# A two-layer hybrid decoder trunk: the post-norms' means taken in two fp32r parts, one small projection tile later, and ScalarE's copies of small tiles moved one place ahead

## The reference

```python
for i in range(DEPTH):
    h = rmsnorm(x, norm_pre[i])
    ...
    x = x + rmsnorm(y, norm_post[i])
    gate = jax.nn.sigmoid(rmsnorm(x, pe_norm[i]) @ pe_w_gate[i])
    x = x + gate * (p[i] @ pe_w_proj[i])
```

## Time and profile before

| | us |
|---|---|
| median of 3 runs | 633.39 (633.24 to 633.53) |
| the profiled execution, its own time | 633.8 |
| its span, first to last instruction | 631.8 |
| TensorE busy | 625.2 (99%) |
| VectorE, ScalarE, GpSimd busy | 391.8, 324.6, 297.7 |
| granted TensorE clock, mean | 1.000 of full speed |

### The profile page before, as it was taken

One profiled execution on the slowest core, in us unless ns is written; L12 is line 12 of the kernel. 1 busy time (PEld: TensorE's weight loads), 2 busy tenths in 40 slices (PEclk: granted clock), 3 DMA queues, 4 the chain that ended last, 5 costly groups with the idle time before them and its releaser, 6 DMA issues.

```text
span 631.8 us, 9261 instructions
## 1 busy us (share of the span) xinstructions
PE 625.2 (99%) x2924; PEld 516.2 (82%) x2924; DVE 391.8 (62%) x787; ACT 324.6 (51%) x562; POOL 297.7 (47%) x400
## 2 busy tenths in 40 slices
PE   8999999999999999999999999999999999999997
PEld 6788888888888887888888888888888888888886
DVE  5688777787868787555969635432424243357874
ACT  7766666565657575565666632321222222566451
POOL 1785463645555457000447458546553742002570
PEclk9999999999999999999999999999999999999999
DMA  6344333434335434155103323323223331352031
GB/s 208 108 161 120 117 130 119 114 114 116 115 121 108 102 104 149 34 166 168 33 25 109 101 75 123 106 95 128 71 98 101 100 133 67 116 184 67 1 133 67
DMA packets 26585, 68.03 MB, mean 108 GB/s; under 512 B 3504, under 2 KB 9648, under 8 KB 26560
## 3 DMA queue, kind: packets, MB, share of 16 engines
q1 hardware_dynamic: 26560, 67.71, 33.6%
HBM read 65.57 MB, written 2.13 MB: 107 GB/s over the span
## 4 chain that ended last, share of the span: by engine, by line
PE 96%; DVE 1%; DMA 1%; issue 1%; ACT 1%; SPq 0%; DVEq 0%
PE ps_pj L1115 26%; PE ps_pj L1117 26%; PE ps_pj L1116 26%; PE ps_tr L1124 3%; PE ps_o L1251 2%; PE ps_sc L1215 2%; PE ps_o L1250 1%; PE ps_sc L1213 1%; PE ps_pj L1152 1%; PE ps_tr L1115 1%; PE ps_tr L1117 1%; PE ps_tr L1116 1%; PE ps_pj L1146 1%; PE ps_pj L1145 1%; DMA xT<-in_xT 1%
## 5 line engine op out<-in xcount | busy, mean ns | idle before, releaser
L431 POOL TENSOR_TENSOR w_lo<-w_raw,w_hi 128x256 fp32r<-128x256 f32 x316 | 242.9, 801 | 129.7 <-ACT w_hi L493 120.9
L1115 PE MATMUL ps_pj<-act_hi,w_hi 128*128 128x512 f32 (+1 forms) x712 | 281.2, 395 | 0.0
L1117 PE MATMUL ps_pj<-act_hi,w_lo 128*128 128x512 f32 (+1 forms) x712 | 276.2, 388 | 0.0
L1116 PE MATMUL ps_pj<-act_lo,w_hi 128*128 128x512 f32 (+1 forms) x712 | 276.0, 388 | 0.0
L1117 PEld LDWEIGHTS ps_pj<-act_hi,w_lo 128*128 128x128 f32 x712 | 133.7, 188 | 27.8
L1115 PEld LDWEIGHTS ps_pj<-act_hi,w_hi 128*128 128x128 f32 x712 | 133.9, 188 | 25.4 <-DVE act_lo L928 0.4
L1116 PEld LDWEIGHTS ps_pj<-act_lo,w_hi 128*128 128x128 f32 x712 | 134.0, 188 | 23.9
L493 ACT CAST w_hi<-w_raw 128x1024 fp32r<-128x1024 f32 x95 | 99.4, 1048 | 87.9 <-DMA w_raw<-in_weights 65.5
L470 POOL TENSOR_TENSOR acc<-acc,sq 128x512 f32<-128x512 f32 x14 | 22.4, 1598 | 116.5 <-ACT sq L661 116.2
L439 POOL TENSOR_TENSOR bias<-bias,mask 128x128 f32<-128x128 f32 x60 | 30.7, 542 | 69.4 <-DMA bias<-negc_scratch 69.4
L563 ACT ACTIVATE logit<-logit,nmax 128x128 f32<-128x128 f32 (+1 forms) x64 | 36.1, 563 | 46.7 <-DVE nmax L828 46.4
(11 more groups left out here) (164 smaller groups left out, 776.4 us busy)
## 6 DMA issues: line engine op xcount, KB each, us to landing
w_raw<-in_weights SPq DMA_DIRECT2D x100, 512.0 KB, 3.3
bias<-negc_scratch SPq DMA_DIRECT2D x15, 256.0 KB, 7.4
bias<-negc_scratch SPq DMA_DIRECT2D x15, 192.0 KB, 6.3
xT<-in_xT SPq DMA_DIRECT2D x8, 256.0 KB, 5.6
bias<-negc_scratch SPq DMA_DIRECT2D x15, 128.0 KB, 5.0
out<-xT SPq DMA_DIRECT2D x7, 256.0 KB, 3.0
p_in<-in_pT SPq DMA_DIRECT2D x2, 512.0 KB, 4.7
bias<-negc_scratch SPq DMA_DIRECT2D x15, 64.0 KB, 3.5
```

The costliest lines, as they stand in the source:

```text
L431: last = nc.gpsimd.tensor_tensor(w_lo[place % RING][:, tiles], w_raw[stream(place) % RAW][:, tiles], w_hi[place % RING][:, tiles], ALU.sub ...
L1115: nc.tensor.matmul(out, w_h, a[0][:, k, tokens], start=k == first, stop=False)
L1116: nc.tensor.matmul(out, w_h, a[1][:, k, tokens], start=False, stop=False)
L1117: end = nc.tensor.matmul(out, w_l, a[0][:, k, tokens], start=False, stop=k == last)
```

## The change

The post-norm's mean takes the two-part form, in both layers. ScalarE rounds `acc` (`acc_round`) ahead of the last weight split, VectorE computes the rest (`acc_rest`) ahead of its last `slot_lo`, and TensorE calls `split_mean` in small tile 6 in place of `norm_mean` in small tile 5. The counts in the other calls follow. ScalarE's copy of small tile 0 now stands ahead of the first `act_hi`, and copies 1, 2 and 3 stand behind `act_hi` 0, 1 and 2, each ahead of the square.

```diff
-PLE_COPY_AT = {0: [0], 1: [1], 2: [2]}
-PLE_COPY_BEHIND = {2: [3]}
+PLE_COPY_AHEAD = [0]
+PLE_COPY_AT = {0: [1], 1: [2], 2: [3]}
...
-NORM_AFTER = KT - 3
+NORM_AFTER = KT - 2
...
                         nc.scalar.copy(p_hi[:], p_in[:]).then_inc(p_hi_done, 1)
+                acc_round(3 * l + 1)
                 weight_hi(SLOT_GATE[l] + 3, SLOT_GATE[l] + 3)
                 norm_scale(3 * l + 1, ps_o[:])
...
+                for tile in PLE_COPY_AHEAD:
+                    ple_copy(tile)
                 for m in range(KT):
                     act.wait_ge(x_new, 2 * KT * l + m + 1)
                     nc.scalar.activation(a_g[:, m, :], xT[:, m, :], ACT.Copy, scale=g_pe[:, l, m:m + 1]
...
                     square(3 * KT * l + KT + m, xT[:, m, :])
-                    for tile in PLE_COPY_BEHIND.get(m, []):
-                        ple_copy(tile)
...
+                acc_rest(3 * l + 1)
                 slot_lo(SLOT_GATE[l] + 3)
...
-                acc_rest(2 * l + 1)
+                acc_rest(3 * l + 2)
...
-                acc_rest(2)
+                acc_rest(3)
...
-            def norm_mean(n):
-
-                pe.wait_ge(acc_done, KT * n)
-                nc.tensor.matmul(ps_o[:], mean_f[:], acc[:], start=True, stop=True).then_inc(ms_done, 1)
...
                         if m == NORM_AFTER and k == 1:
-                            norm_mean(3 * l + 1)
+                            split_mean(3 * l + 1)
...
-                split_mean(2 * l + 1)
+                split_mean(3 * l + 2)
...
-                                 between={KT - 3: lambda: split_mean(2)}, lead=True)
+                                 between={KT - 3: lambda: split_mean(3)}, lead=True)
```

## The result

The changed kernel takes 635.66 us, a median over 22 runs (634.70 to 639.35); the kernel before takes 633.66 in the same sessions (22 runs, 632.77 to 636.71). The ratio is 1.0035, with a 95% interval of 1.0025 to 1.0046. Forecast were 635.3 us and a ratio of 1.0031.

What follows compares the result with a forecast made beforehand. TensorE, busy 625.2 of 631.8 us, was taken as the bound, meeting VectorE's chain at the seventh k. A mean 0.97 us later per layer adds 1.94 to 633.39, the saving being waited away: 635.3 us, range 634.2 to 636.7.

Steps and rivals of the forecast that it cites:

- The meeting point: At the seventh k, TensorE's stream and VectorE's chain arrive together; TensorE loses 0.05 us there.
- The mean's time: Six more small matmuls stand ahead of the mean, so its result comes 0.97 us later in each layer.
- the cover: At the mean, both parts of acc are ready about 0.45 us before TensorE comes, so it doesn't wait.
- The saving: On TensorE, the two-part mean takes 0.47 us against 0.86: 0.39 us saved a layer, going into waiting.
- The displaced work: ScalarE's weight split, VectorE's w_lo and the next weight tile's DMA move later behind the insertions and cost nothing.
- The copies: ScalarE's moved copies of the small tiles are worth 0; the first fits ahead of the first act_hi.
- the gap: ScalarE's idle time before the first act_hi, 1.54 us, takes the 0.59 us copy; without it, 0.5 us cost.
- The sum: TensorE is released 0.97 us later in each layer, 1.94 us in all, giving 635.3 us, +0.31%.
- The third rival: VectorE and GpSimd fall into another step: no change (chance 0.08), 634.3 us (0.07) or more (0.05).
- The second rival: acc_hi, acc_lo or displaced w_lo comes late at the mean, about +0.7 us a layer: 636.7 us, chance 0.10.
- the exclusion that it cites: A two-SBUF-input VectorE instruction and a GpSimd one reading SBUF exclude each other wholly; the first to start wins.
- the likeliest case: The whole chain shifts by 0.97 us a layer: 635.3 us, own range 634.9 to 636.1, chance 0.66.

Runs made afterwards that it cites:

- small adds: GpSimd's adds cut to 8 of 512 columns, result not computed: in the changed kernel 632.65 us, ratio 0.9985; in the kernel before 633.43 us, 0.9994.
- copies alone: Kernel before with ScalarE's copies at the new places, f32 mean left in tile 5: 635.82 us, ratio 1.0039.
- the mean in tile 5 and new copies: Changed kernel with the two-part mean put back to small tile 5, copies at the new places: 636.97 us, ratio 1.0054.
- adds moved: Changed kernel with GpSimd's adds of squares 5, 6 and 7 taken by VectorE behind its chain: 633.38 us, ratio 0.9998.

## Why the prediction was right

**The meeting point.** The step on which all hung was that TensorE's stream and VectorE's chain arrived together at the seventh k, from one loss of 0.05 us. The small adds show it: taking the chain away is worth 0.07 us a layer before and 28.37 - 26.92 = 1.45 after. The copies alone show it from another side, with TensorE's stream unchanged.

**The mean's time.** Predicted 0.97 us later, measured 0.96 at the first `t_a`. TensorE didn't wait for `acc_lo`; the cover was 0.51 us, predicted 0.45. The clock times named as signs (the Ln at 301.35, `t_a` at 302.6, the seventh `act_lo` done at 322.2) came as 300.84, 302.11 and 321.69: each is right once the 0.50 us is added by which this profile was early at the anchor.

**The saving.** Predicted 0.39 us a layer and swallowed by the wait; measured 0.40 where nothing swallows it. The wait grew by 0.98 + 0.40 = 1.38 us a layer, predicted 0.97 + 0.39 = 1.36. The profile counts 1.8 us a layer of idle weight loads, which overstates it, since the loads run ahead of the matmuls: ahead of the fifth k the load stands 0.27 us and the matmuls lose 0.11 (0.34 us apart in place of 0.23).

**The displaced work.** `w_lo` of 299.93 ended at 301.15, before the chain began at 302.11. It cost nothing. As for the DMA behind it, the profile of the changed kernel has no wait of TensorE for a DMA in either stretch.

**The copies.** Worth 0 here, as predicted. What was too small is the price without the gap: I wrote 0.5 us, the copy's length, but the copy also waits for small tile 0, and with the mean on time the cost is 1.13. The experiment's own expectation had 1.2 to 1.3. The sum wasn't touched, because the late mean makes the gap.

**GpSimd.** The adds met the same VectorE instructions. The third rival didn't occur, and the lengths of VectorE's disturbed rows agree to 0.01 us. The second rival didn't either. In its rows the prediction read only VectorE's wait for GpSimd, but the exclusion that it cites holds here in both directions: GpSimd waits for VectorE in the same way (last section). That left the sum alone, as every start moved alike.

**The size.** 1.94 us predicted, 1.97 in the two stretches, and 2.2 by the ratio (1.6 to 2.9). The range of the likeliest case has a slip: 0.3 a layer and half of 0.38 a layer add to 1.0 for both layers, not 0.8. Nothing hung on it, since neither cost occurred.

## What to carry to other kernels

A wait of almost nothing on the bounding engine can mark the place where two chains meet; trace the other chain back before taking work off this engine, since a saving that makes the other chain start later costs its whole lateness. The edit that pays is then on the chain that arrives last: here, moving three of GpSimd's adds off VectorE's way gave back 1.1 us a layer with the arithmetic unchanged. And when an instruction is put into another's waiting time, look at what it waits for itself: the same copy was free behind a late mean and cost 1.1 us a layer behind a timely one.

## What the hardware showed beyond that

VectorE and GpSimd exclude each other in both directions, and a row's length follows from what was running when it started. There are 100 full-width adds by GpSimd in the residual chains of the eight kernels that have such adds. In 96 of them GpSimd started while VectorE was in an `xT` addition or an `act_lo`, both of which read two tensors in SBUF. These adds ended 1.13 to 1.17 us behind the end of that VectorE instruction, whatever was left of it, and so took 1.39 to 1.79 us. The other four started during a `t_a`, which reads one tensor in SBUF and `ps_o` in PSUM, and took 1.30 or 1.31. In the other direction, the first `xT` addition or `act_lo` that started inside an add ended 0.53 to 0.56 us behind the add. An undisturbed `xT` addition takes 0.69 us and an undisturbed add 1.30, so all but some 0.15 us of either is held back (an estimate from these rows).

This explains the longer addition in the two kernels where ScalarE held the first `act_hi` back. There the first add starts during a `t_a`, and the fourth `xT` addition starts 0.50 us into it, where it was 1.04 or 1.05 in the changed kernel and the one before. It waits for more of the add, and takes 1.35 or 1.36 us in place of 1.07 or 1.08. Here is the kernel with the mean in tile 5 and new copies. The first add ends at 585.23 and the addition 0.55 behind it, at 585.78; the second add started 0.23 us before that, and ends 1.16 behind it:

```profile
583.93 1.30 POOL L470 TENSOR_TENSOR acc<-acc,sq 128x512 f32<-128x512 f32 x1 [56.20 <-ACT sq L661]
584.43 1.35 DVE L994 TENSOR_TENSOR xT<-xT,t_a 128x512 f32<-128x512 f32 x1
585.55 1.39 POOL L470 TENSOR_TENSOR acc<-acc,sq 128x512 f32<-128x512 f32 x1 [0.32 <-ACT sq L661]
```

The profiles also differ by up to 2.5 us ahead of any edit: the last add of the output projection in layer 0 starts at 296.70 in one kernel (copies alone) and at 299.23 in another (adds moved), whose TensorE had a granted clock of 0.98 in its first 100 us and 0.996 over the whole span, where the others had 0.998 or more. A comparison of spans from one profile each can thus be wrong by as much as the effect.
